# The recurrence's diagonal from elementwise products and a matrix of ones, and five-tile attention scores as two parts of 320 columns

## What is computed

```
x = x + 1/2 * SwiGLU_1(RMSNorm(x))
P = RMSNorm(x) @ W_in            -> attn q,k,v | hgrn q,f,i,g   (512 columns each)
attention (8 heads x 64): a chunk of 64 frames sees itself and 8 chunks before it, plus a bias
recurrence (4 heads x 128): S_t = diag(f_t) S_{t-1} + (1-f_t) i_t^T,  o_t = S_t^T q_t
x = x + concat(attention, recurrence) @ W_out
x = x + 1/2 * SwiGLU_2(RMSNorm(x))
```

## Time and profile before

| | |
|---|---|
| Time, median of 3 runs | 1889.31 us (1888.82 to 1889.9) |
| The profiled execution: its own time, its span | 1889.1 us, 1887.5 us |
| Granted TensorE clock, mean | 1.000 |
| PE matmul busy | 1869.3 us, 99% |
| DVE, ACT, POOL busy | 1126.6, 676.1, 406.1 us |
| Level 0 of the four heads, PE busy (L928) | 7.8 us |
| Attention scores, 512 columns, PE busy (L1021) | 22.6 us |

### The profile page before, as it was taken

How to read it: one execution, slowest core, us unless ns; L and a number is a source line. 1 busy time by engine, 2 the same in 40 slices (tenths; PEclk the granted TensorE clock), 3 DMA queues, 4 the chain that set the end, 5 groups by cost and what they waited for, 6 DMA issues and landing times. The chain is left out here.

```text
span 1887.5 us, 24459 instructions
## 1 busy us (share of the span) xinstructions
PE 1869.3 (99%) x9171; PEld 1545.9 (82%) x9171; DVE 1126.6 (60%) x1591; ACT 676.1 (36%) x1029; POOL 406.1 (22%) x319
## 2 busy tenths in 40 slices
PE   9999999999999999999999999999999999999999
PEld 8888888888888888888888667888888888888887
DVE  6966666665556641156667773377666656655464
ACT  7423323233334533210223663353323333333332
POOL 2043422341103110002222310000434222411030
PEclk9999999999999999999999999999999999999999
DMA  5355444437866433324343410133554454368653
GB/s 182 112 201 184 145 169 161 161 129 253 312 198 191 133 129 122 138 90 139 133 139 111 150 60 1 68 112 112 195 184 151 155 174 148 142 238 309 219 193 139
DMA packets 221341, 296.52 MB, mean 157 GB/s; under 512 B 15377, under 2 KB 117913, under 8 KB 221234
## 3 DMA queue, kind: packets, MB, share of 16 engines
q1 hardware_dynamic: 206752, 262.19, 40.8%
q0 software_dynamic: 6272, 18.14, 2.9%
q10 hardware_dynamic: 8210, 14.75, 2.0%
HBM read 206.13 MB, written 92.56 MB: 158 GB/s over the span
## 5 line engine op out<-in xcount | busy, mean ns | idle before, releaser
L710 PE MATMUL ps<-hThi,whi 128*128 128x512 f32 x888 | 346.6, 390 | 0.2 <-DVE hid L1735 0.2
L712 PE MATMUL ps<-hThi,wlo 128*128 128x512 f32 x888 | 345.6, 389 | 0.0
L711 PE MATMUL ps<-hTlo,whi 128*128 128x512 f32 x888 | 345.6, 389 | 0.0
L710 PE MATMUL ps<-whi 128*128 128x512 f32 x616 | 240.0, 390 | 0.0
L712 PE MATMUL ps<-whi,wlo 128*128 128x512 f32 x616 | 239.7, 389 | 0.0
L711 PE MATMUL ps<-wlo,whi 128*128 128x512 f32 x616 | 239.7, 389 | 0.0
L710 PEld LDWEIGHTS ps<-hThi,whi 128*128 128x128 f32 x888 | 166.7, 188 | 35.1 <-issue 0.9
L712 PEld LDWEIGHTS ps<-hThi,wlo 128*128 128x128 f32 x888 | 166.7, 188 | 34.7
L711 PEld LDWEIGHTS ps<-hTlo,whi 128*128 128x128 f32 x888 | 166.7, 188 | 34.1
L710 PE MATMUL ps<-hXhi,whi 128*128 128x512 f32 x480 | 186.9, 389 | 0.7 <-issue 0.7
L712 PE MATMUL ps<-hXhi,wlo 128*128 128x512 f32 x480 | 186.8, 389 | 0.0
(11 more groups left out here) (218 smaller groups left out, 2827.9 us busy)
## 6 DMA issues: line engine op xcount, KB each, us to landing
hid_scratch<-hid SPq DMA_DIRECT2D x132, 256.0 KB, 3.3
raw<-ffn_w_gate SPq DMA_DIRECT2D x44, 512.0 KB, 3.7
raw<-ffn_w_up SPq DMA_DIRECT2D x44, 512.0 KB, 4.9
wdb<-ffn_w_down SPq DMA_DIRECT2D x44, 512.0 KB, 4.1
wd_scratch<-wdb SPq DMA_DIRECT2D x88, 256.0 KB, 4.3
raw<-hid_scratch SPq DMA_DIRECT2D x80, 256.0 KB, 2.7
rawx<-hid_scratch SPq DMA_DIRECT2D x74, 256.0 KB, 2.8
raw<-w_in SPq DMA_DIRECT2D x28, 512.0 KB, 5.0
```

The costliest lines, as they stand in the source:

```text
L710: pe.matmul(dst, ahi, bhi, start=first, stop=False, skip_group_check=onto)
L711: pe.matmul(dst, ahi, blo, start=False, stop=False, skip_group_check=onto)
L712: return pe.matmul(dst, alo, bhi, start=False, stop=last, skip_group_check=onto)
```

## The change

Level 0 no longer multiplies on PE. DVE makes the elementwise product of keys and queries into `aT` (two instructions), ACT copies it with rounding into `diag_high`, DVE subtracts to get `diag_low` (both 128 x 1024 float32r), and PE multiplies a 128 x 128 matrix of ones by them: two matmuls of 512 columns into each of the banks 0 and 1. Every row of the result then holds the column sums; `keep_scores(0)` is unchanged. `diag_low` lies where `aT` is and `diag_high` where `st` is. The semaphore of level 0 (`scaled`) now comes from the subtraction. ACT waits for the products and copies at the start of a group, ahead of its first evacuation.

Five-tile scores are two parts of 320 columns, each at the start of its bank, and DVE reads them with a pattern of 2 x 320. Three semaphores of `lb` become one, and DVE sets `ones` once before the projection's second group.

```
@@ right side of SBUF
+            ones = keep("ones", [P, P], F32R, c, "right")
+            keep("clear_of_fF_to_tot", [P, 7 * T], where=c, side="right")
+            diag_low = keep("diag_low", [P, T], F32R, c, "right")
+            keep("clear_of_kS", [P, T], where=c, side="right")
+            diag_high = keep("diag_high", [P, T], F32R, c, "right")
@@ TensorE, hgrn(j), level 0
                             pe.wait_ge(ro_ready, j + 1)
-                            for c in range(TT):
-                                mm = pe.matmul(ps[:, c * P:(c + 1) * P], hK[:, c * P:(c + 1) * P],
-                                               fQ[:, c * P:(c + 1) * P], start=True, stop=True)
+                            for h in range(2):
+                                at = slice(h * HALF, (h + 1) * HALF)
+                                pe.matmul(bank(h), ones[:, :], diag_high[:, at], start=True, stop=False)
+                                mm = pe.matmul(bank(h), ones[:, :], diag_low[:, at], start=False, stop=True)
@@ TensorE, before the first head
+            pe.wait_ge(mask_set, LEVELS)
@@ TensorE, scores(w)       (SPLIT = BAND // 2 = 320)
-                    for c, m in ((c0, min(n * P, HALF - c0)), (HALF, c0 + n * P - HALF)):
+                    if n == KEY_TILES:
+                        pieces = ((0, 0, SPLIT), (SPLIT, HALF, SPLIT))
+                    else:
+                        pieces = ((c0, c0, min(n * P, HALF - c0)), (HALF, HALF, c0 + n * P - HALF))
+                    for c, at, m in pieces:
...
-                                last[hd] = pe.matmul(ps[:, b + c:b + c + m], qT[rows, p % 2, t * P:(t + 1) * P],
+                                last[hd] = pe.matmul(ps[:, b + at:b + at + m], qT[rows, p % 2, t * P:(t + 1) * P],
@@ ScalarE, group(...)
+                if head is not None:
+                    act.wait_ge(diag_made, head + 1)
+                    act.activation(diag_high[:, :], aT[:, :], ACT.Copy).then_inc(diag_hi, 1)
                 for o in range(7):
                     evac(n0, advn, o, func)
@@ VectorE, before the second group
+            dve.tensor_scalar(ones[:, :], ident[:, :], 0.0, 1.0, ALU.mult, ALU.add).then_inc(mask_set, 1)
@@ VectorE, head(j)
                 link(dve.tensor_scalar(k[:, :, 0, :], f[:, :, 0, :], -1.0, 1.0, ALU.mult, ALU.add))
-                dve.tensor_scalar(k[:, :, 1, :], f[:, :, 1, ::-1], -1.0, 1.0, ALU.mult, ALU.add).then_inc(scaled, 1)
+                link(dve.tensor_scalar(k[:, :, 1, :], f[:, :, 1, ::-1], -1.0, 1.0, ALU.mult, ALU.add))
                 dve.wait_ge(read_done, j + 1)
+                q = fQ[:, :].rearrange("p (a par t) -> p a par t", par=2, t=P)
+                kq = aT[:, :].rearrange("p (a par t) -> p a par t", par=2, t=P)
+                link(dve.tensor_tensor(kq[:, :, 0, :], k[:, :, 0, :], q[:, :, 0, :], ALU.mult))
+                dve.tensor_tensor(kq[:, :, 1, :], k[:, :, 1, ::-1], q[:, :, 1, :], ALU.mult).then_inc(diag_made, 1)
                 link(dve.tensor_tensor(hQ[:, :], fQ[:, :], fF[:, :], ALU.mult))
+                dve.wait_ge(diag_hi, j + 1)
+                dve.tensor_tensor(diag_low[:, :], aT[:, :], diag_high[:, :].bitcast(F32), ALU.subtract).then_inc(scaled, 1)
                 pair_keys(1)
@@ VectorE, attention, reading the scores
+                        if n == KEY_TILES:
+                            dst, shift = (a.rearrange("p (two c) -> p two c", two=2)
+                                        for a in (S[:, v % SLOTS, :], bias[:, p % 2, hd, :]))
+                            src = ps[:, b:b + 2 * HALF].rearrange("p (two c) -> p two c", two=2)[:, :, 0:SPLIT]
```

More of the change, by code:

```diff
@@ L171 @@
 SLOTS = 4
+SPLIT = BAND // 2
 OUT_STEPS = NU // 2
@@ L319, in build @@
             mk = keep("mk", [P, (LEVELS - 1) * HALF], U8, c, "right")
+            ones = keep("ones", [P, P], F32R, c, "right")
             sso = keep("sso", [P, TT], where=c, side="right")
             rso = keep("rso", [P, TT], where=c, side="right")
+        with ExitStack() as c:
+            keep("clear_of_fF_to_tot", [P, 7 * T], where=c, side="right")
+            diag_low = keep("diag_low", [P, T], F32R, c, "right")
+            keep("clear_of_kS", [P, T], where=c, side="right")
+            diag_high = keep("diag_high", [P, T], F32R, c, "right")
         with ExitStack() as c:
@@ L430, in build @@
         proj_stored = [sem(f"proj_stored{s}") for s in range(2)]
-        lb_diff = sem("lb_diff")
-        lb_sig = sem("lb_sig")
-        lb_ready = sem("lb_ready")
+        lb_step = sem("lb_step")
         sig_ready = sem("sig_ready")
@@ L484, in build @@
         cat_loaded = sem("cat_loaded")
+        diag_made = sem("diag_made")
+        diag_hi = sem("diag_hi")
         pool_passed = sem("pool_passed")
@@ L1483, in _ @@
             group(0, 0, ACT.Silu, True)
-            act.wait_ge(lb_diff, 1)
-            act.activation(lb[:, 0, :], lb[:, 2, :], ACT.Sigmoid).then_inc(lb_sig, 1)
-            act.wait_ge(lb_ready, 1)
+            act.wait_ge(lb_step, 1)
+            act.activation(lb[:, 0, :], lb[:, 2, :], ACT.Sigmoid).then_inc(lb_step, 1)
+            act.wait_ge(lb_step, 3)
             group(1, 0, ACT.Sigmoid, True)
@@ L1927, in _ @@
             dve.wait_ge(lb_loaded, 16)
-            dve.tensor_tensor(lb[:, 2, :], lbs[:, 0, :], lbs[:, 1, :], ALU.subtract).then_inc(lb_diff, 1)
+            dve.tensor_tensor(lb[:, 2, :], lbs[:, 0, :], lbs[:, 1, :], ALU.subtract).then_inc(lb_step, 1)
             dve.wait_ge(setup_moved, 16)
@@ L1946, in _ @@
                 split(P_MIX + 4 + q)
-            dve.wait_ge(lb_sig, 1)
-            dve.tensor_scalar(lb[:, 1, :], lb[:, 0, :], -1.0, 1.0, ALU.mult, ALU.add).then_inc(lb_ready, 1)
+            dve.wait_ge(lb_step, 2)
+            dve.tensor_scalar(lb[:, 1, :], lb[:, 0, :], -1.0, 1.0, ALU.mult, ALU.add).then_inc(lb_step, 1)
             for n in (1, 2):
@@ L2058, in read_out @@
                    .then_inc(ro_ready, 1)
-            per_head = 5 + 5 * 7 + 2 * 6
+            per_head = 7 + 5 * 7 + 2 * 6
             dve.wait_ge(ext_stored, 16)
@@ L2107, in _ @@
                         b = score_bank(v) * HALF
[L2108 to L2111, removed]
+                        if n == KEY_TILES:
+                            dst, shift = (a.rearrange("p (two c) -> p two c", two=2)
+                                        for a in (S[:, v % SLOTS, :], bias[:, p % 2, hd, :]))
+                            src = ps[:, b:b + 2 * HALF].rearrange("p (two c) -> p two c", two=2)[:, :, 0:SPLIT]
+                        else:
+                            dst, shift = S[:, v % SLOTS, c0:c0 + n * P], bias[:, p % 2, hd, BAND - n * P:BAND]
+                            src = ps[:, b + c0:b + c0 + n * P]
+                        last = dve.tensor_tensor_reduce(dst, src, shift, -1.0, 3.0e38, ALU.add, ALU.min,
+                                                        nmax[:, hd, t:t + 1])
                     last.then_inc(unit_max, 1)
```

## The result

| | before | changed |
|---|---|---|
| Time, median | 1889.36 us (6 runs, 1888.82 to 1889.95) | 1897.6 us (6 runs, 1895.95 to 1900.41) |
| Mean granted clock of the runs | 1.000 in all | 0.996 to 1.000 |
| The profiled execution: its time, its span | 1889.1, 1887.5 us | 1897.22, 1895.6 us |

The ratio is 1.0047, 95% interval 1.0036 to 1.0058: slower, by 8.9 us (6.8 to 11.0). The forecast was 1894.5, with a range up to 1897.8. The median of the six runs lies 0.2 us inside that range; the ratio of 1.0047 puts the time at 1898.2, above it. The sign, the chain ahead of level 0 and the collision with POOL were right. The size was short by 3.7 us, since the sum had nothing for the clock.

A forecast was written before the change was run, and what follows sets the result against it. TensorE, busy 99% of the span, was taken as the bound. 1889.1 us + 2.9 (level 0 late, less PE's gain and filled waits) + 2.3 (POOL's collision) gave 1894.5 us, range 1890.5 to 1897.8.

The forecast's parts named there:

- The sign: Whole kernel: slower than before, given a chance of 0.62, against 0.31 for the same and 0.07 for faster.
- The gain: Level 0 on PE: four float32r matmuls take 0.91 us instead of 1.79, saving 0.88 us a head, 3.5 for four.
- The chain ahead of level 0: Products, ACT's copy, subtraction in series: PE waits 2.54 us (2.0 to 3.1) in three heads, not the first.
- POOL meets the subtraction: Second and third heads: DVE and POOL exclude each other, one loss of 2.3 us or two of 1.2: +2.3 us.
- The fourth head's waits: Levels 2 and 3 of the fourth head: later PE fills 1.2 of the 1.7 us it had waited for DVE.
- Attention: Five-tile scores as two parts of 320 columns: no change in time, 0 us (bounds -1.6 and +2.5).
- The clock: Rival: PE's clock falls to 1.2 GHz behind a wait of 4.9 us, giving 1897.5 us; chance 0.05.
- The rival's price: Clock rival: each us of work at 1.2 GHz costs one more, so a drop of 3 us gives 1897.5 us.

The follow-up runs named there:

- pe_only: Kernel before, its DVE and ACT order kept, with level 0 as four float32r ones matmuls on old columns: 1886.38 us, ratio 0.9986.
- rec_only: Changed kernel without its attention part (five-tile scores again 512 + 128 columns): 1897.5 us, ratio 1.0044 to before.
- after_again: The changed kernel timed once more, unaltered, for the spread of its executions: 1899.65 us, ratio 1.006 to before.
- shift: Changed kernel with levels 0 and 1 one place later in PE's order: 1892.84 us, ratio 1.0024 to before.
- chain_only: Changed chain on DVE and ACT, while PE makes level 0 with before's eight float32 matmuls: 1902.53 us, 13.5 more than before.

## Why the prediction was wrong

Point by point, the profiled execution against the steps:

- **The gain** of 0.88 us a head: right (57.0 us a head against 57.9 in `pe_only`; four matmuls 0.23 us apart).
- **The chain ahead of level 0**: right in the profiled execution. The subtraction was put 4.75 us behind L2056 and starts 4.73 behind; the wait was put at 2.54 and is 2.55, 2.55 and 2.45 us. The first head waits not at all, as forecast.
- **POOL meets the subtraction**: right in kind and price. Of the two forms, 2.3 us once or 1.2 twice, the profile has the second, with 1.25 and 1.2 us; `rec_only`'s has the first, in two heads, and `after_again`'s one of each. POOL's place varies from execution to execution (4.81 and 4.88 us behind L2056 here, 4.68 in `rec_only`), so this sum has no fixed value. The Trainium skill's rule in "SBUF — State Buffer", section "SBUF: two separate sides", that whoever starts first holds the shared ports for a whole instruction, is borne out at 0.05 us and at 0.08 us of lead, with 3.36 and 1.22 us for the same subtraction.
- **The fourth head's waits**: 1.2 us taken back, 1.3 measured by the distances between starts (1.0 by the list).
- **Attention**: 0 forecast, 0 measured.
- **The clock**: this step failed. The sum had nothing for it; I gave it a chance of 0.05, and only behind a wait of 4.9 us. It fell in 15 of 16 executions, with up to four stretches of 3.4 us in one, and in the traces behind 10 of 12 waits of 2.4 to 2.6 us and all four of 4.6 to 4.7. A stretch costs some 1.6 us, or 0.4 where it fills the wait at level 1. The rival's price was off as well: it put 3 us on a drop of 3 us, but in a stretch at half the clock half of the time is lost, not all. From the start of the recurrence to attention the profiled execution is 7.1 us longer than before; without its one stretch 5.5, where I had 5.2. The rest to the 8.1 us of span lies outside the recurrence, within before's own spread (1888.2 to 1890.7). The two executions at the median have three stretches each, by their clock of 0.997.

The mistake was to price a long wait only by its length. I knew that PE would stand still for 2.5 us three times, longer than the longest wait between matmuls in the recurrence before, and that no row showed what the clock does then; so the bound of each such wait should have been its length plus a fall, and the range 5 us wider above. The prediction also took the 40 nines of rows 1 for a full clock in every slice, which they don't show; the mean of 1.000 does.

The Trainium skill's "TensorE: Matmul & The Clock Gate", section "HAM oscillation — how this bites in real kernels", describes gaps that bring the clock down again and again. The traces agree in kind, with three falls in `after_again`'s. The gaps that the page warns of are longer than these; here 2.7 to 2.8 us between two starts were enough, and the measurement decides.

What stays open: why the same wait of 2.5 us brings a fall in one head and none in another (the second and third head of the profiled execution had none), and so how many stretches an execution gets. `shift`'s four runs at 0.999 have no trace.

## What to carry to other kernels

An edit that takes work off the busiest engine and gives it to others must be read at the semaphore that it now waits for: 0.88 us saved on PE stood behind 3.9 us of chain with 1.45 us of room. Where the engine's order is written by hand, the same edit wants its places moved with it: with seven levels (four in the last head) and POOL's two products put elsewhere, the loss of 8 to 11 us became a gain of 3.4. And a wait of TensorE of a few microseconds is to be priced with a fall of the clock on top: at full clock the changed kernel lost 6.6 us, with the falls up to 14. That the clock never fell is to be read from its mean, not from the digits of the page.

## What the runs showed of the hardware

- Behind 14 of 16 waits of 2.4 to 4.7 us in six traces the granted clock went to 1.2 GHz, in 12 of them for 3.4 us, from 0.1 us ahead of the first matmul behind the wait to 1.4 us after it. In the other two (the third heads of `rec_only` and `chain_only`, waits of 4.7 and 4.6 us) it fell 1.3 and 2.1 us before the wait ended and stayed down for 6.8 us. Behind waits of 1.25 us it did not fall, in any trace.
- A float32 copy of DVE from SBUF to SBUF, one operand only, is held up by POOL's product just as a two-operand instruction is: 5.00 us for two copies of 0.3. The products with the identity, which read PSUM and SBUF, ran beside the same POOL instruction unharmed in 0.69 us.
